# A two-block transformer kernel on one core: three instead of two pairs of weight chunks per column group go through seven products in the first network

## The reference

```python
hn = rmsnorm(h, ffn_norm[l])
h = h + (jax.nn.silu(hn @ w_gate[l]) * (hn @ w_up[l])) @ w_down[l]
```

## Time and profile before

| | |
|---|---|
| time, median of 3 runs | 2334.25 us (2334.05 to 2334.6) |
| profiled execution, span | 2333.0 us |
| outside the span, by the median | 1.25 us |
| TensorE (PE) busy | 2315.2 us, 99%, 11296 matmuls |
| VectorE (DVE) busy | 1619.8 us, 69% |
| ScalarE (ACT) busy | 1244.4 us, 53% |
| first network, gate and up | about 603 to 1077 us of the span |
| first network, w_down | about 1077 to 1322 us |

### The profile page before, as it was taken

One profiled execution on the slowest core, in us unless ns is written; L12 is line 12 of the kernel. 1 busy time (PEld: TensorE's weight loads), 2 busy tenths in 40 slices (PEclk: granted clock), 3 DMA queues, 4 the chain that ended last, 5 costly groups with the idle time before them and its releaser, 6 DMA issues.

```text
span 2333.0 us, 29072 instructions
## 1 busy us (share of the span) xinstructions
PE 2315.2 (99%) x11296; PEld 1953.5 (84%) x11296; DVE 1619.8 (69%) x2291; ACT 1244.4 (53%) x1847; POOL 21.2 (1%) x34
## 2 busy tenths in 40 slices
PE   9999999999999999999999999999999999999998
PEld 7888888888888888888888888888888888888887
DVE  6445565665787787786565677977888888885444
ACT  7445454555655555555454567866444444444343
POOL 1000000000000000000000000000000000000000
PEclk9999999999999999999999999999999999999999
DMA  8665555656655656656656666455666666666665
GB/s 270 192 188 172 156 172 153 187 184 189 217 180 186 220 171 202 214 165 194 208 188 194 210 187 185 147 160 176 193 189 192 190 190 189 192 189 192 195 192 162
DMA packets 226425, 439.29 MB, mean 188 GB/s; under 512 B 13632, under 2 KB 17888, under 8 KB 225904
## 3 DMA queue, kind: packets, MB, share of 16 engines
q1 hardware_dynamic: 224400, 429.51, 59.6%
q0 software_dynamic: 1888, 7.93, 1.1%
HBM read 435.24 MB, written 2.15 MB: 187 GB/s over the span
## 4 chain that ended last, share of the span: by engine, by line
PE 95%; DVE 3%; ACT 1%; issue 1%; DMA 0%; SPq 0%; DVEq 0%; POOLq 0%; POOL 0%; ACTq 0%
PE bank L1757 22%; PE bank L1755 22%; PE bank L1756 22%; PE bank L1805 14%; PE bank L1807 7%; PE bank L1817 2%; PE bank L1725 2%; PE bank L1728 2%; PE bank L1726 2%; DVE wlo L1147 1%; ACT whi L796 1%; DMA raw<-in_w_in_dram 0%; PE bank L1860 0%; ACT S2b L1033 0%; PE bank L1877 0%
## 5 line engine op out<-in xcount | busy, mean ns | idle before, releaser
L1147 DVE TENSOR_TENSOR wlo<-raw,whi 128x1024 fp32r<-128x1024 f32 (+2 forms) x660 | 801.8, 1216 | 566.1 <-ACT whi L796 565.0
L796 ACT CAST whi<-raw 128x1024 fp32r<-128x1024 f32 (+2 forms) x660 | 688.2, 1043 | 871.0 <-PE bank L1757 618.4
L1805 PE MATMUL bank<-TT,whi 128*128 128x512 f32 x1408 | 488.9, 391 | 0.8 <-DVE TT L1409 0.8
L1755 PE MATMUL bank<-whi,TT 128*128 128x512 f32 (+1 forms) x1172 | 461.3, 394 | 1.7 <-DVE wlo L1147 1.0
L1757 PE MATMUL bank<-whi,TT 128*128 128x512 f32 (+1 forms) x1172 | 454.5, 388 | 0.0
L1756 PE MATMUL bank<-wlo,TT 128*128 128x512 f32 (+1 forms) x1172 | 453.9, 387 | 0.0
L1807 PE MATMUL bank<-TT,wlo 128*128 128x256 f32 x1408 | 394.1, 280 | 0.0
L1805 PEld LDWEIGHTS bank<-TT,whi 128*128 128x128 f32 x1408 | 263.3, 187 | 58.9 <-issue 1.3
L1807 PEld LDWEIGHTS bank<-TT,wlo 128*128 128x128 f32 x1408 | 266.1, 189 | 0.0
L1755 PEld LDWEIGHTS bank<-whi,TT 128*128 128x128 f32 x1172 | 220.2, 188 | 46.2 <-DVE wlo L1147 1.9
L1757 PEld LDWEIGHTS bank<-whi,TT 128*128 128x128 f32 x1172 | 219.9, 188 | 45.4
(11 more groups left out here) (298 smaller groups left out, 3028.7 us busy)
## 6 DMA issues: line engine op xcount, KB each, us to landing
raw<-in_ffn_w_up_dram SPq DMA_DIRECT2D x176, 512.0 KB, 3.6
raw<-in_w_in_dram SPq DMA_DIRECT2D x120, 512.0 KB, 3.7
raw<-in_w_down_dram SPq DMA_DIRECT2D x88, 512.0 KB, 4.7
raw<-in_ffn_w_down_dram SPq DMA_DIRECT2D x88, 512.0 KB, 4.7
RX<-in_w_gate_dram SPq DMA_DIRECT2D x66, 512.0 KB, 4.0
RX<-in_w_up_dram SPq DMA_DIRECT2D x66, 512.0 KB, 4.2
raw<-in_swa_w_in_dram SPq DMA_DIRECT2D x48, 512.0 KB, 3.7
raw<-in_w_out_dram SPq DMA_DIRECT2D x32, 512.0 KB, 4.0
```

Of the source, the lines that this page charges most:

```text
L796: eng.copy(parted(hi_at(u), src), src).then_inc(s_cast, 1)
L1147: eng.tensor_tensor(parted(lo_at(u), src), src, parted(hi_at(u), src).bitcast(F32), ALU.subtract).then_inc(s_lo, 1)
L1755: eng.matmul(o, lh[:, ts], hi[:, kk, :], start=start, stop=False)
L1805: eng.matmul(o[:, :], hi[:, kk, fs], TT[:, k, :, :].rearrange("p a s -> p (a s)"), start=k == 0, stop=False)
```

## The change

`SUMS` becomes (0, 1, 2): three pairs of each group go through seven products, and five plain ones remain for gate and up. The work of a seven-product pair is cut anew, into kinds C, B, F and H. The partial products that go through up's second bank are no longer begun afresh for each kind: the bank runs on (C, B, F, H, then the plain chunks of up), and it is read between the kinds (three `snap` copies in place of four). Its last content stays there as part of up's second half, so up's second half is emptied by one instruction (L1234, `HID<-bank,RS,SG`) in place of two. VectorE's `sum` is now two instructions: one difference of two copies (L1467), and one that reads the bank itself (L1471), for which the plain chunks of up wait.

The buffers are laid out anew: gate and up chunks of the three pairs go to `PB`, six blocks of 512 columns per pair, in which the sums are also made (`add0` L1454, three per group; `add1` L1457 and `add2` L1461, one each per group over all three pairs). Plain chunks use the four `raw` buffers in place of three `RX`. `weight_loads` gives the order of the fetches, which now differs from that of use: the six fetches of the next group stand behind up's third, fourth and fifth plain chunk, and those of group 0 among the output projection's. `WX` gets memory of its own, and the scratch for software DMA descriptors is set to 4096.

The diff, cut to its core (empty lines left out):

```diff
-SUMS = (0, 1)
-PLAIN = (2, 3, 4, 5, 6, 7)
+SUMS = (0, 1, 2)
+PLAIN = (3, 4, 5, 6, 7)
+NS = len(SUMS)
...
+def weight_loads(chunks):
+    at = network_chunks(chunks)
+    rows = list(range(OUT + 8))
+    for t in range(OUT + 8, FFN):
+        rows.append(t)
+        if (t - OUT - 8) % 3 == 0 and (t - OUT - 8) // 3 < 2 * NS:
+            half, c = divmod((t - OUT - 8) // 3, NS)
+            rows.append(at[("gate", "up")[half], 0, SUMS[c]])
...
+    for f in range(NF):
+        turn = [at["gate", f, p] for p in PLAIN] + [at["up", f, p] for p in PLAIN]
+        more = [[] for _ in turn]
+        if f < NF - 1:
+            more[7] = [at["up", f + 1, p] for p in SUMS]
+            more[8] = [at["gate", f + 1, p] for p in SUMS[:2]]
+            more[9] = [at["gate", f + 1, p] for p in SUMS[2:]]
+        for t, z in zip(turn, more):
+            rows += [t] + z
+    rows += range(DN, END)
+    assert sorted(rows) == list(range(END))
+    return rows
...
+        plain = [("w", at["gate", f, p]) for p in PLAIN]
+        gate, up = ([at[st, f, p] for p in SUMS] for st in ("gate", "up"))
+        rows += plain[:1] + [("C", t) for t in gate]
+        rows += plain[1:2] + [("B", t) for t in gate[::2]]
+        rows += plain[2:3] + [("F", t) for t in up]
+        rows += plain[3:4] + [("H", t) for t in gate]
+        rows += plain[4:] + [("w", at["up", f, p]) for p in PLAIN]
...
-            for c in range(2):
-                put(FFN - 1 + c, "add0", c)
-                put(FFN - 1 + c, "add1", c)
-        for j in range(4):
-            put(g[2 + j], "snap", 4 * f + j)
+            for c in range(NS):
+                put(FFN - 1, "add0", c)
+            put(FFN - 1, "add1", 0)
+        put(g[1], "add2", f)
+        for j in range(3):
+            put(g[1 + j], "snap", 3 * f + j)
         if f:
             for b in range(2):
-                put(g[2 + b], "htr", 2 * f - 2 + b)
-                put(g[3 + b], "hsp", 2 * f - 2 + b)
+                put(g[1 + b], "htr", 2 * f - 2 + b)
+                put(g[2 + b], "hsp", 2 * f - 2 + b)
+        put(g[3], "sum", 2 * f)
+        put(g[4], "sum", 2 * f + 1)
         put(u[1], "silu", f)
-        put(g[5], "sum", 2 * f)
-        put(u[1], "sum", 2 * f + 1)
         if f < NF - 1:
-            for c in range(2):
-                put(u[2 + 2 * c], "add0", 2 * f + 2 + c)
-                put(u[3] if c == 0 else num["gate", f + 1, PLAIN[1]], "add1", 2 * f + 2 + c)
+            for c in range(NS):
+                put(u[2 + min(c, 1)], "add0", NS * (f + 1) + c)
+            put(u[4], "add1", f + 1)
     for b in range(2):
...
+        PB = at("PB", rH, 13312, [NS, 6, 512])
         FH = at("FH", rH, 11264, [6, 2, 2, S], F32R)
...
+                    f, j = divmod(i, 3)
+                    ends = ("C", num["gate", f, SUMS[-1]]), ("B", num["gate", f, SUMS[::2][-1]]), ("F", num["up", f, SUMS[-1]])
+                    ac.wait_ge(s_mm, step_of[ends[j]] + 1)
                     if f == 0:
+                        ac.wait_ge(s_ex, NS)
                     else:
+                        ac.wait_ge(*emptied_at(("gate", f - 1), j // 2))
+                        ac.wait_ge(*emptied_at(("up", f - 1), 0))
                     copy(ST[:, j, :], bank[banks["up", f][1]][:, :]).then_inc(s_snap, 1)
...
+                        ve.wait_ge(*emptied_at(("up", i - 1), 1))
+                        ve.wait_ge(s_hd, i)
+                    ve.wait_ge(s_snap, 3 * i + 3)
                     eng.tensor_tensor(SG[:, 0, :], b[0][:, :], ST[:, 0, :], ALU.add).then_inc(s_emptyV, 1)
                     eng.tensor_tensor(SG[:, 1, :], b[1][:, :], ST[:, 2, :], ALU.add).then_inc(s_emptyV, 1)
                 elif st == "up":
-                    h0, h1 = HID[:, i % 2, 0, :], HID[:, i % 2, 1, :]
                     if i >= 2:
                         ve.wait_ge(s_htr, 2 * (i - 2) + 2)
-                    ve.wait_ge(s_sum, 4 * i + 4)
-                    eng.tensor_tensor(h1, b[1][:, :], ST[:, 3, :], ALU.add).then_inc(s_emptyV, 1)
-                    eng.tensor_tensor(h0, b[0][:, :], ST[:, 1, :], ALU.add).then_inc(s_emptyV, 1)
                     ve.wait_ge(s_silu, 2 * i + 2)
-                    for z in (1, 0):
-                        ve.wait_ge(*emptied_at(g, z))
-                        eng.scalar_tensor_tensor(out=HID[:, i % 2, z, :], in0=HID[:, i % 2, z, :], scalar=rs_2[:, z:z + 1],
-                                                 in1=SG[:, z, :], op0=ALU.mult, op1=ALU.mult).then_inc(s_hd, 1)
+                    eng.scalar_tensor_tensor(out=HID[:, i % 2, 1, :], in0=b[1][:, :], scalar=rs_2[:, 1:2],
+                                             in1=SG[:, 1, :], op0=ALU.mult, op1=ALU.mult).then_inc(s_emptyV, 1)
+                    ve.wait_ge(s_sum, 2 * i + 2)
+                    eng.tensor_tensor(HID[:, i % 2, 0, :], b[0][:, :], ST[:, 1, :], ALU.add).then_inc(s_emptyV, 1)
+                    ve.wait_ge(*emptied_at(g, 0))
+                    eng.scalar_tensor_tensor(out=HID[:, i % 2, 0, :], in0=HID[:, i % 2, 0, :], scalar=rs_2[:, 0:1],
+                                             in1=SG[:, 0, :], op0=ALU.mult, op1=ALU.mult).then_inc(s_hd, 1)
...
+                elif name == "add0":
+                    f, c = divmod(i, NS)
+                    for st in ("gate", "up"):
+                        n = num[st, f, SUMS[c]]
+                        ve.wait_ge(l_raw[rslot[n]], 16 * raw_load[n])
+                    if f:
+                        ve.wait_ge(s_lo, step_of["H", num["gate", f - 1, SUMS[c]]] + 1)
+                    z = PB[:, c, :, :]
+                    eng.tensor_tensor(z[:, 0:5:4, :], z[:, 4:6, :], z[:, 2:5:2, :], ALU.subtract).then_inc(s_ta, 1)
+                elif name == "add1":
+                    ve.wait_ge(s_ta, NS * i + NS)
+                    eng.tensor_tensor(PB[:, :, 1, :], PB[:, :, 5, :], PB[:, :, 0, :], ALU.subtract).then_inc(s_tb, 1)
+                elif name == "add2":
+                    ve.wait_ge(s_tb, i + 1)
+                    ve.wait_ge(s_lo, step_of["C", num["gate", i, SUMS[-1]]] + 1)
+                    eng.tensor_tensor(PB[:, :, 3, :], PB[:, :, 3, :], PB[:, :, 1, :], ALU.subtract).then_inc(s_tc, 1)
+                elif name == "sum":
+                    f, j = divmod(i, 2)
+                    if j == 0:
+                        ve.wait_ge(s_snap, 3 * f + 3)
+                        eng.tensor_tensor(ST[:, 1, :], ST[:, 1, :], ST[:, 2, :], ALU.subtract).then_inc(s_sum, 1)
                     else:
+                        ve.wait_ge(s_sum, 2 * f + 1)
+                        ve.wait_ge(s_mm, step_of["H", num["gate", f, SUMS[-1]]] + 1)
+                        eng.tensor_tensor(ST[:, 1, :], bank[banks["up", f][1]][:, :], ST[:, 1, :],
+                                          ALU.add).then_inc(s_sum, 1)
...
                 if kind == "C":
+                    products = ((up, 1, rows(k, 0)), (gate, 0, rows(k + 1, 0)))
                 elif kind == "B":
+                    pe.wait_ge(s_snap, 3 * f + 1)
+                    products = tuple((up, 1, sums_of_rows(z, 2)) for z in cs_)
+                elif kind == "F":
+                    pe.wait_ge(s_snap, 3 * f + 2)
+                    products = ((up, 1, sums_of_rows(c, 3)), (up, 0, sums_of_rows(c, 4)))
                 else:
+                    pe.wait_ge(s_snap, 3 * f + 3)
+                    products = ((up, 1, sums_of_rows(c, 1)), (gate, 1, rows(k + 1, 1)))
                 for b, (g, half, (lh, ll)) in enumerate(products):
                     fresh = begins(g, half)
+                    o, chain = bank[banks[g][half]], (g, half) == (up, 1)
+                    read = chain and cs_[-1] == NS - 1 and (kind != "B" or b == len(cs_) - 1)
+                    eng.matmul(o[:, :], lh, hi[:, b, :], start=fresh, stop=False, skip_group_check=chain)
+                    eng.matmul(o[:, :], lh, lo[:, b, :], start=False, stop=False, skip_group_check=chain)
+                    mm = eng.matmul(o[:, :], ll, hi[:, b, :], start=False, stop=read, skip_group_check=chain)
                 mm.then_inc(s_mm, 1)
...
                 if st == "up":
-                    pe.wait_ge(s_snap, 4 * i + 4)
+                    pe.wait_ge(s_sum, 2 * i + 2)
...
+    nc = _bacc.Bacc("TRN2", target_bir_lowering=False, num_devices=1, dynamic_dma_scratch_size=4096)
```

More of the change, by code:

```diff
@@ L139, in raw_slots @@
 def raw_slots(chunks):
-    slot, before, load, used, loads = [], [], [], {}, {}
-    for t in range(END):
-        if FFN <= t < DN:
-            p = chunks[t][2] // 2
-            if p in SUMS:
-                z = 2 * SUMS.index(p) + (chunks[t][0] == "up")
-            else:
-                z = min((4, 5, 6), key=lambda x: used.get(x, x - 100))
-        else:
-            z = min(range(RAW), key=lambda x: used.get(x, x - 100))
-        slot.append(z)
-        before.append(used.get(z))
-        used[z] = t
+    slot, before, load, used, loads = [0] * END, [None] * END, [0] * END, {}, {}
+    for n, t in enumerate(weight_loads(chunks)):
+        p = chunks[t][2] // 2
```

(20 more changed lines are left out.)

161 lines of the change are left out of this document (56 added, 105 removed).

## The result

The changed kernel takes 2368.68 us in the median (2366.29 to 2370.83, four runs), the kernel before beside it 2334.43 us: ratio 1.0136, interval 1.0115 to 1.0157. It is slower, as forecast, but by 34 us and not by 15; the range ended at 2356. The profiled execution has a span of 2364.5 us, 31.5 more than before.

A forecast was written before the change was run, and what follows sets the result against it. TensorE was taken to bound the kernel; -7.48 + 12.8 + 5.2 + 4.7 = +15.2 us gave a forecast of 2349.4 us, 0.65% slower. The range was 2343.6 to 2356 us.

The forecast's parts named there:

- matmuls removed: One product less per group on TensorE, 3 matmuls in each of 11 groups at 0.2267 us: -7.48 us.
- place 1: Groups 1 to 10: C0 waits 1.28 us for VectorE to empty up's second bank (L1234), ten times: +12.8 us.
- place 2: All 11 groups: unit u3 waits 0.47 us for the new bank-reading sum (L1471) behind a subtraction: +5.2 us.
- place 3: Group 0: C0 waits for its bank's emptying (L1220), behind added weight sums on VectorE: +4.7 us.
- end of the network: Up's first bank was to be free 0.06 us later than before, costed at nothing.
- What bounds the kernel: TensorE, busy 99% of 2333.0 us: time is matmuls times start distance, unless something new makes TensorE wait.
- The fetches ... just in time: 0: Six chunks up to next group's g3: 7.7 us of transfer in about 10; 0, at most 0.6 us per group.
- The rival was priced at +6.0: Late fetches: g3's chunk lands late, place 1 starts up to 0.6 us later, ten times: 2355.4 us; 0.10 with dearer sums.
- Edits costed at nothing: Third pair's activation sums, snaps, up's first bank at the network's end, and descriptor scratch: no cost.
- The clock: Rival: TensorE falls to half clock after place 3's long wait, 2 to 5 us more: 2351.7 to 2354.0 us; chance 0.08.
- named signs of being wrong: C0's wait absent, VectorE gaps between C0's subtraction and L1234, or the clock below 1.00.
- The bank source: Skill page's longer fixed term for bank reads: 0.065 us per wait, 1.4 us in all; not added, trace disagreed.

The follow-up runs named there:

- e5: Changed kernel with the next group's paired-chunk fetches issued two plain chunks earlier, at most two in a row: 2367.69 us, ratio 1.0120, network 500.37 us.
- e4: Kernel before with only WX moved to memory of its own at the changed kernel's address, and descriptor scratch of 4096: 2340.26 us, ratio 1.0034.
- e10: Changed kernel with only WX's place changed, to right behind wlo: 2371.04 us, ratio 1.0160, network 512.84 us.
- e3: Changed kernel with the emptying of up's banks, and the sum that reads the bank, ahead of the subtraction due at the same step: 2351.53 us, ratio 1.0073.
- e2: Changed kernel with group 0's weight sums made three to six chunks earlier: 2368.79 us, ratio 1.0139.
- e17: Changed kernel with both the spread fetches and WX right behind wlo: 2362.93 us, ratio 1.0100, network 496.76 us.
- e1: Changed kernel with 32 bytes of filling ahead of WX, nothing else: 2365.44 us, ratio 1.0136.
- e14: Kernel before with WX in memory of its own at byte 204928 and descriptor scratch of 4096: 2334.76 us, one run.
- e13: Kernel before with WX in memory of its own at byte 184448 and descriptor scratch of 4096: 2343.28 us, one run.

## Why the prediction was wrong

The table goes by the profiled executions (span +31.5 us), from start to start of matmuls.

| term | forecast, us | measured, us | how measured |
|---|---|---|---|
| matmuls removed | -7.5 | -7.5 | 11263 |
| place 1 | +12.8 | +15.9 | ten waits |
| place 2 | +5.2 | +6.1 | eleven waits |
| place 3 | +4.7 | +4.7 | one wait |
| end of the network | 0 | +1.2 | one wait for L1237 |
| WX's place | 0 | +5.7 | distances below 0.30, against those before |
| second matmul behind a wait | 0 | +1.6 | starts of about 0.31: 41 for 21 |
| half clock | 0 | +4.0 | 15 starts over 0.40, and transposes |
| sum | +15.2 | +31.7 | of 31.7 in the network and its end |

- **What bounds the kernel, and the direction**: right. The three places, their counts and their lines came as worked out; the emptying at the end of a group was what the edit had to be held against. Place 3 was right to the tenth, rows and all; the sum of 1536 columns took 1.75 us, 1.67 from start to start, as taken.
- **"The fetches ... just in time: 0"**: the first step that failed. Transfers landed late at the ends of nine groups. This is most of what place 1 has over 12.8 (e5: 13.5), and with it the wait at 658.07 is 1.87 us long and the clock falls behind it (e5: 1.52 us, no fall). I took six chunks as 7.7 us of transfer, at the largest rate in the trace, in about 10 us, and the median landing, and did not follow one chunk through SyncE's queue. In group 5 it took 11.85 us from u6's issue (817.28) to the landing of g3's chunk (829.13). The rival was priced at +6.0; e5 took 4.5 off the network. Its chance, 0.10 together with another, was too low.
- **"Edits costed at nothing"**: the second. WX's move was not in the list as a cost at all; alone it costs 5.5 us (e4), and 5.7 by this trace, 3.5 of it at matmuls that stream WX and the rest at the others. It is the largest term that the sum lacked. At the end of the network the first bank was not free "0.06 later": L1237 stood behind a subtraction and L1234, and a unit of w_down waited 1.1 us. The activation sums and the snaps did cost nothing.
- **The clock**: the sum had it at nothing. The rival's place was right, and its size too (+2 to 5 us after place 3; 2.4 there, 1.6 more in the second stretch); its chance of 0.08 was too low. A clock below 1.00 was also among the named signs of being wrong. Nothing spoke against it: the wait of place 3 was forecast longer than any before. Given such a wait it belonged into the sum. That a wait of 1.87 us can do it too, I had not reckoned with; e10 shows it after five of 1.81 to 2.74. But the length alone does not decide: one of 2.06 (e10, 845.75), one of 1.86 (e3) and one of 2.94 (e2, 791.96) left the clock alone.
- **Place 2** was short by 0.08 us per wait (0.55 for 0.47), and the first matmul behind a wait holds the next one off for 0.31 us where I had 0.2267: two small terms, 2.5 us in all, that recur with each stop.
- **The range** took each of these as a case by itself. They came together, and some feed the next: a late landing lengthens the wait, and the longer wait can cost clock. What remains open is that the changed kernel's other three runs took 1.3 to 4.5 us more than the profiled one, at the same mean granted clock of 0.997; no trace of them was taken.
- **The bank source**: the trace of the changed kernel doesn't bear out the Trainium skill's rule (page "VectorE: DVE Perf Modes", section "The TRN2 errata") either: L1227, from a bank, takes 0.68 us, and so does L1467, from SBUF alone.

## What to carry to other kernels

When an edit makes the bounding engine wait where it never did, the wait is not the whole price: add the 0.31 us of the first matmul behind each stop, and leave room for matmuls at half clock (here about 1.6 us each time behind some of the waits of 1.8 us and more). A tile that is only moved is an edit too: give it the remainder of the other tiles in the ring, and try the move alone. And before a faster engine is put ahead of late transfers, mend the transfers: the same move of WX gained nothing in e10, and 3.6 us of network from e5 to e17. An order on one queue is cheap to mend: here a few changes of order and one of place turned +34 us into -5.

## What the runs showed of the hardware that was not expected

- Matmuls of 512 columns of f32 that stream a tile at remainder 992 or 1024 modulo 2048 bytes start 0.232 to 0.236 us apart, at remainder 128 0.227, whether the tile lies low or high in the partition (three places against seven). All other tiles of the ring had the remainder 128. Even its neighbours on other tiles slow a little, to as much as 0.230.
- The granted clock falls to half at waits of 4.5 us and behind some of 1.81 to 2.98 us (the changed kernel, e1, e2, e10), for seven or eight matmuls, and not behind others as long (2.94 us in e2); with the transposes between, TensorE works at it for 5 us at place 3.
- The second network of this kernel runs at either of two rates, 1700 or 1732 matmuls in 300 us, at a granted clock of 1.00 in both, in variants of the kernel before (e14, e13) as in those of the changed one. What sets it was not tried.
